# Context work placed between the latents' scan steps, lag blocks ahead of the chunk sums

## What is computed

```python
def token_mixer(h, h0_f, h0_b, rows, p):
    z = h @ p["w_in"]
    u, cb, cc, ch = jnp.split(z, [D_SSM, D_SSM + D_CONV, D_SSM + 2 * D_CONV], axis=-1)
    y_ssm, h_f, h_b = ssm_mixer(u, h0_f, h0_b, p)     # two complex diagonal scans, gelu, GLU
    y_conv = cb * short_conv(cc * ch, p["conv_w"], p["conv_b"], rows)
    y_ssm, y_conv = rmsnorm(y_ssm, ...), rmsnorm(y_conv per head, ...)
    return jnp.concatenate([y_ssm, y_conv], axis=-1) @ p["w_out"], h_f, h_b

def layer(x, cond, h0_f, h0_b, rows, p):
    sh1, sc1, g1, sh2, sc2, g2 = modulation(cond, p["w_mod"], p["b_mod"])
    y, h_f, h_b = token_mixer(rmsnorm(x, norm1) * (1 + sc1) + sh1, ...)
    x = x + g1 * y
    h = rmsnorm(x, norm2) * (1 + sc2) + sh2
    return x + g2 * peer(h, ...), h_f, h_b
```

## Time and profile before

| | us |
|---|---|
| median of three executions | 1924.85 |
| the profiled execution | 1922.27 |
| its span | 1920.1 |
| TensorE busy in the span | 1194.3 (62%) |
| VectorE busy | 1382.6 (72%) |
| ScalarE busy | 373.5 (19%) |
| GpSimd busy | 725.1 (38%) |
| HBM traffic, mean over the span | 396 GB/s |

### The profile page before, as it was taken

The page is one execution under the profiler, slowest core; times in us unless marked ns, Lnnn a source line. Parts: engine busy times, 40 slices in busy tenths (PEclk is TensorE's granted clock), DMA queues, the critical chain, the costliest instruction groups (busy, mean ns, idle before and its releaser), DMA issues.

```text
span 1920.1 us, 21154 instructions
## 1 busy us (share of the span) xinstructions
PE 1194.3 (62%) x7716; PEld 475.8 (25%) x7716; DVE 1382.6 (72%) x3664; ACT 373.5 (19%) x845; POOL 725.1 (38%) x666
## 2 busy tenths in 40 slices
PE   6989898999777777775543343544343454444434
PEld 3569644444322322221110000111000011111001
DVE  8968567777766766669777776677777678766664
ACT  5142441121122121111211110121111121111110
POOL 0000233344444434445434444444444354444440
PEclk9999999999878877775755555565555565555555
DMA  9855699999999999999999999999999999999994
GB/s 372 328 209 199 257 395 414 378 416 420 390 421 399 419 422 421 420 389 422 420 422 423 421 421 421 421 421 421 422 422 421 421 421 418 422 420 421 418 420 182
DMA packets 120968, 753.16 MB, mean 392 GB/s; under 512 B 12240, under 2 KB 27856, under 8 KB 33568
## 3 DMA queue, kind: packets, MB, share of 16 engines
q0 software_dynamic: 92160, 671.13, 84.5%
q1 hardware_dynamic: 28704, 80.69, 11.0%
HBM read 749.12 MB, written 11.04 MB: 396 GB/s over the span
## 4 chain that ended last, share of the span: by engine, by line
DMA 43%; PE 28%; DVE 23%; issue 2%; POOL 1%; ACT 1%; SPq 0%; DVEq 0%; POOLq 0%; ACTq 0%
DMA r<-table,gidx 31%; DVE r L1747 9%; DMA mix_r<-table,gidx 8%; PE bank L878 7%; PE bank L846 6%; PE bank L983 3%; DMA r<-w_mod 3%; DVE mix_r L1747 2%; PE bank L996 2%; PE bank L813 1%; POOL r L1935 1%; PE bank L962 1%; PE bank L855 1%; DVE i L1680 1%; PE bank L788 1%
## 5 line engine op out<-in xcount | busy, mean ns | idle before, releaser
L1935 POOL DMA_INDIRECT r<-table,gidx x542 | 607.7, 1121 | 865.3 <-PE bank L878 723.9
L1747 DVE CUSTOM_DVE_ANT_0 r<-r 128x1024 f32<-128x1024 f32 x542 | 658.1, 1220 | 246.5 <-DMA r<-table,gidx 246.0
L878 PE MATMUL bank<-r,cond 128*32 128x512 f32 x1432 | 327.2, 911 | 370.4 <-DVE cond L1759 295.2
L878 PE MATMUL bank<-r,wgt 128*32 128x512 f32 x736 | 166.8, 921 | 194.1 <-DVE wgt L1759 145.8
L1289 ACT ACTIVATE r<-r 128x2 f32<-128x2 f32 x320 | 65.1, 204 | 1013.1 <-DVE r L1747 1012.5
L878 PEld LDWEIGHTS bank<-r,cond 128*32 128x32 f32 x1432 | 37.1, 129 | 572.0 <-DVE cond L1759 437.2
L1935 POOL DMA_INDIRECT mix_r<-table,gidx x98 | 109.4, 1116 | 136.1 <-PE bank L878 117.0
L1747 DVE CUSTOM_DVE_ANT_0 mix_r<-mix_r,r 128x1024 f32<-128x1024 f32 x98 | 119.3, 1221 | 48.4 <-DMA mix_r<-table,gidx 48.2
L878 PE MATMUL bank<-mix_r,cond 128*32 128x512 f32 x264 | 91.1, 994 | 80.7 <-DVE cond L1759 63.4
L846 PE MATMUL bank<-hT_r,r 128*128 128x512 f32 x256 | 121.5, 630 | 0.9 <-ACT hT_r L1143 0.9
L878 PEld LDWEIGHTS bank<-r,wgt 128*32 128x32 f32 x736 | 18.9, 130 | 295.3 <-DVE wgt L1759 214.3
(11 more groups left out here) (367 smaller groups left out, 1637.1 us busy)
## 6 DMA issues: line engine op xcount, KB each, us to landing
r<-w_mod SPq DMA_DIRECT2D x24, 1024.0 KB, 9.7
r<-wq_heads SPq DMA_DIRECT2D x14, 1024.0 KB, 8.8
r<-table,gidx POOLq DMA_INDIRECT x542, 18.7
wq_heads<-w_query SPq DMA_DIRECT2D x8, 1024.0 KB, 12.1
r<-w_tiles SPq DMA_DIRECT2D x12, 512.0 KB, 7.8
x_r<-w_tiles SPq DMA_DIRECT2D x10, 512.0 KB, 6.0
hT_r<-xT SPq DMA_DIRECT2D x4, 640.0 KB, 6.1
r<-w_u SPq DMA_DIRECT2D x1, 2048.0 KB, 29.5
```

What stands on the lines that cost most here:

```text
L878: last = mm(bank[ACC[b % 2][h]][to:to + TG, :], pair_weights(NPR * G + g)[:, e, :], rows[SLOT[G * TOPK + k]][:, D + h * 512:D + (h + 1) * ...
L1747: V.tensor_tensor_reduce(row, row, h2r[tg], 1.0, 0.0, ALU.mult, ALU.add, hid[:, par, k:k + 1]).then_inc(dot_done, 1)
L1935: G_.indirect_dma_start(rows[SLOT[j]], None, table, bass.IndirectOffsetOnAxis(gidx[:, e, k:k + 1], 0)).then_inc(row_in[SLOT[j]], 16)
```

## The change

In the order of the kernel:

- **SP.** `load_mod(18)` and `(19)` stay, then come `load_conv_ctx(6)` and `(7)`, then the two `wt` loads, then `load_mod(20)` and `(21)`, `load_conv_ctx(8)` and `(9)`, `load_mod(22)` and `(23)`. The wait for `zc_mm` 2 ahead of `wt` goes.
- **PE.** The lag blocks' matmuls stand ahead of the chunk sums. Slabs 20 to 22 leave the selections of M; slab 20 stands behind `conv_ctx(0)`, which stands ahead of the context's scan outputs, and slabs 21 to 23 ahead of `conv_ctx(2)`. The GLU follows `conv_ctx(1)` and those slabs. The head sums and their spread come right behind it, `out_ctx` begins with the convolution's channels, and all eight `y_lat` stand between `scores(0)` and `spread_experts(0)`.
- **ScalarE.** Of chunk sums 8 to 15 it takes the even ones. The copy of `ccx` stands ahead of that of `Hbc`, the convolution's squares and root ahead of the GLU's sigmoid, the copy to `Hb` behind `take_scores(0)`.
- **VectorE.** It takes the odd chunk sums (`s_back`), copies the lag blocks ahead of the scan, and makes the imaginary products in one instruction with reversed halves instead of two. The context's convolution, norms and gating stand between the latents' steps (after steps 8, 11, 12, 14 and 15). Segment 2 follows them, segment 3 lies around the second root, and segment 4 comes after `xsc_ready`.

```diff
@@ sync @@
             for q in range(2):
                 load_conv_ctx(q)
-            for n in range(18, 24):
-                load_mod(n)
-            sp.wait_ge(zc_mm, 2)
+            load_mod(18)
+            load_mod(19)
+            for q in range(6, 8):
+                load_conv_ctx(q)
             for j in range(2):
                 sp.dma_start(wt[:, j, :, :], w_tiles[NCONV + j]).then_inc(wtg_in, 16)
-            for q in range(6, 8):
+            load_mod(20)
+            load_mod(21)
+            for q in range(8, 10):
                 load_conv_ctx(q)
+            load_mod(22)
+            load_mod(23)
             sp.wait_ge(m_mm, 2)
             sp.dma_start(wqa, w_query[:, :, 0:DQ]).then_inc(ld_first, 16)
-            for q in range(8, 10):
-                load_conv_ctx(q)
             sp.wait_ge(mod_mm, 24)
             sp.dma_start(woA, w_o[:, 0:4, :, :]).then_inc(ld_wo, 16)
             for q in range(10, 12):
@@ tensor @@
-            pe.wait_ge(bpt_ev, 17)
-            for g in range(16):
-                if g >= 2:
-                    pe.wait_ge(s_ev, g - 1)
+            def chunk_sums(g):
+
+                if g >= 10 and g % 2:
+                    pe.wait_ge(s_back, (g - 9) // 2)
+                elif g >= 2:
+                    pe.wait_ge(s_ev, min(g - 1, 4 + g // 2))
...
+            pe.wait_ge(bpt_ev, 17)
+            for g in range(8):
+                chunk_sums(g)
+            mod_slab(17)
+            for g in range(8, 16):
+                chunk_sums(g)
             mod_slab(18)
             mod_slab(19)
...
-                mod_slab(20 + a)
-            mod_slab(22)
...
+            pe.wait_ge(m_ev, 1)
+            conv_ctx(0)
+            mod_slab(20)
             pe.wait_ge(m_ev, 8)
             pe.wait_ge(hbc_ready, 1)
...
-            conv_ctx(0)
+            conv_ctx(1)
             pe.wait_ge(yc_gelu, 2)
...
+            mod_slab(21)
+            mod_slab(22)
             mod_slab(23)
-            conv_ctx(1)
+            conv_ctx(2)
...
             mod_turn(2)
-            conv_ctx(2)
+            head_sums()
+            spread_heads()
...
             pe.wait_ge(ld_wo, 32)
-            out_ctx(True, range(KS), 1)
-            out_ctx(False, range(KS, KD), 2)
+            out_ctx(True, range(KS, KD), 1)
+            out_ctx(False, range(KS), 2)
             pe.wait_ge(sqc_ready, 3)
             token_sums(257, sqx[0], True, False)
-            pe.wait_ge(hb_ready, 1)
-            pe.wait_ge(mod_free, 6)
-            y_lat(0, 0)
             pe.wait_ge(sqc_ready, 4)
             token_sums(257, sqx[1], False, True)
-            y_lat(0, 1, range(1))
             spread_root(1)
-            y_lat(0, 1, range(1, 5))
...
             first_query()
             scores(0)
-            y_lat(0, 2)
-            y_lat(0, 3)
-            for i in range(4):
-                y_lat(1, i)
+            pe.wait_ge(hb_ready, 1)
+            pe.wait_ge(mod_free, 6)
+            for n in range(2):
+                for i in range(4):
+                    y_lat(n, i)
             spread_experts(0)
@@ vector @@
-                link(tt(ta, prev, re, ALU.mult),
-                     tt(tb[:, :, 0, :], prev[:, :, 1, :], im[:, :, 0, :], ALU.mult),
-                     tt(tb[:, :, 1, :], prev[:, :, 0, :], im[:, :, 1, :], ALU.mult))
+                link(tt(ta, prev, re, ALU.mult), tt(tb, prev[:, :, ::-1, :], im, ALU.mult))
...
+            lag_blocks()
+            for g in range(9, 16, 2):
+                pr = g % 8 * 2
+                dve.wait_ge(s_mm, g + 1)
+                for r in range(2):
+                    src = bank[4 + g % 2][:, 0:4 * NCH].rearrange("p (q r c) -> p c r q", q=2, r=2)[:, :, r, :]
+                    V.tensor_copy(HH[:, NCC:0:-1, r, 1, pr:pr + 2], src[:, 0:NCC, :])
+                    last = V.tensor_copy(HH[:, NCH - 1:NCC:-1, r, 1, pr:pr + 2], src[:, NCC + 1:NCH, :])
+                last.then_inc(s_back, 1)
...
-                if i == 3:
-                    lag_blocks()
...
+            advance_rest(1, 9)
             dve.wait_ge(ccx_ev, 1)
             dve.wait_ge(zc_mm, 8)
...
+            advance_rest(9, 12)
+            dve.wait_ge(zc_mm, 12)
+            tt(mixc[:, KS:KD, :].rearrange("p k t -> p (k t)"), cvx.rearrange("p k t -> p (k t)"), bank[2][:, :], ALU.mult).then_inc(cvx_ev, 1)
+            advance_rest(12, 13)
...
+            residual_ctx(0)
+            residual_ctx(1)
+            segment_products(3)
             dve.wait_ge(rms_c, 3)
             V.reciprocal(inv1[1], rt1[1]).then_inc(inv_ready, 1)
             gains(4, COL_N2, 6)
+            segment_add(3)
+            segment_store(3)
             dve.wait_ge(inv_mm, 3)
...
             last.then_inc(xsc_ready, 1)
+            segment_products(4)
+            segment_add(4)
+            segment_store(4)
+            V.tensor_copy(small[:, 2:3], eps_c[:, :]).then_inc(scan_lat, 1)
```

More of the change, by code:

```diff
@@ L633, in _ @@
                 last.then_inc(s_mm, 1)
-                if g == 7:
-                    mod_slab(17)
             pe.wait_ge(bd_ready, 1)
@@ L647, in _, with conv_ctx @@
                 last.then_inc(k_mm, 1)
+            pe.wait_ge(bpt_ev, 17)
[4 more added lines that the diff above has]
+                chunk_sums(g)
             mod_slab(18)
             mod_slab(19)
+            def conv_ctx(r):
+                for i in range(4):
+                    q = 4 * r + i
+                    pe.wait_ge(wtc_in[WTC[q]], WTC[:q + 1].count(WTC[q]) * 16)
+                    for k in range(KD):
+                        last = mm(bank[r][:, i * P:(i + 1) * P], wtc[WTC[q]][:, k, :], hT[:, k, 0:CTX], start=(k == 0), stop=(k == KD - 1))
+                    last.then_inc(zc_mm, 1)
             pe.wait_ge(k_ev, 1)
-            pe.wait_ge(s_ev, 16)
+            pe.wait_ge(s_ev, 12)
+            pe.wait_ge(s_back, 4)
             for a in range(2):
@@ L1201, in _ @@
             act.wait_ge(bp_ready, 2)
-            for g in range(16):
+            for g in (*range(8), *range(8, 16, 2)):
                 d, pr = g // 8, (g % 8) * 2
@@ L1590, in _, with advance_rest @@
             rest = slice(1, NJ)
-            for i in range(1, SEG):
-                link(advance(seg[:, rest, i - 1, :, :], seg[:, rest, i, :, :], many_a, many_b, spread(AR, NJ - 1), spread(AI, NJ - 1)))
+            def advance_rest(lo, hi):
+                for i in range(lo, hi):
+                    link(advance(seg[:, rest, i - 1, :, :], seg[:, rest, i, :, :], many_a, many_b, spread(AR, NJ - 1), spread(AI, NJ - 1)))
             def segment_products(j):
```

95 lines of the change are left out of this document (39 added, 56 removed).

## The result

| | before | after |
|---|---|---|
| median of four executions, us | 1924.14 | 1961.3 |
| the profiled execution, us | 1922.27 | 1964.01 |
| its span, us | 1920.1 | 1962.2 |
| first gather issued, us | 215.58 | 254.73 |
| from there to the end of the span, us | 1704.5 | 1707.5 |

The kernel became slower by 37.2 us, estimated as a ratio of 1.0199 with an interval of 1.0181 to 1.0216 (the medians alone give 1.0193). Predicted were 1955, from 1938 to 1964, so the time lies in the range, near its upper end. In the profiled execution the first gather comes 39.15 us later; 30.5 were predicted. The sign and the main places were right, and the size was too small: by 6.7 us against the medians, and by 8.6 in the traces. The two differ because the profiled execution of after lies 2.7 us over the median of its four and that of before 1.9 us under its own.

The account below looks back on a forecast made before the run. The prediction took the DMA-bound expert stage to move with its first gather. That gather comes 30.5 us later, 23.8 before X and 6.7 behind; against the median of 1924.85 this gave 1955 us, range 1938 to 1964.

Parts of the forecast that it names:

- X: End of the scaling in the context's second normalisation, ahead of the key search: predicted at 223.6 us against 199.8 before.
- Lag blocks, chunk sums: Start of the context stage: lag matmuls first, VectorE sharing chunk sums; scan starts at 121.5 us instead of 117.5.
- the ceiling: Upper bound of 6.1 us for chunk-sum groups 8 to 15; the floor was 4.1 and the sum took 5.0.
- Lead and lag cancel: Context scan starts later but loses 3.1 us of lag copies and wait, so it ends at 136.8, where it ended before.
- the low end: Low case of the forecast's own range: faster landings, full clock and no gap, 18.7 us later, 1943.5 us.
- Merged products: Context scan on VectorE: one full-width product for two halves saves 0.06 us of a 0.98 us step.
- This decides: Loads moved on SP's queue: slab 20 issued at 140.6, landing at 148.0, so TensorE stands for 8.7 us.
- Behind X: From the second norm's scaling to the first gather: 22.5 us instead of 15.8, a new wait of 6.7 us.
- rival B: Half clock also behind X (4.4 us more), slab 20 landing in 10.9, groups 8 to 15 unchanged: 1964 us; chance 0.13.
- A: Rival: the loads TensorE waits for arrive in time; first gather 6.9 us later, 1931.8 us; chance 0.13.
- C: Rival: the expert stage gives time back, up to 22 us, for a faster kernel at 1910 us; chance 0.04.
- D: Rival: no effect, waits absorbed before X and the expert stage pays the rest, within 0.2%; chance 0.04.

Follow-up runs that it names:

- e8: Kernel before with only the lag blocks ahead of the chunk sums and the odd half of the last chunk sums on VectorE: 1926.85 us, ratio 1.0019.
- e7: Kernel before with only the merged imaginary products (one full-width product with reversed halves instead of two): 1921.81 us, ratio 0.9993.
- e2: Changed kernel with loads of slabs 20 to 23 and tiles 10 and 11 drawn ahead, mod_slab(21) moved next to mod_slab(20): 1943.54 us, ratio 1.0093.
- e4: Changed kernel with all 15 latents' steps ahead of the context's convolution, segments 2 to 4 behind it, and the copy to Hb early: 1954.94 us, ratio 1.0162.
- e11: Changed kernel with unread matmuls in four TensorE waits (ahead of slab 20, tile 10 and the first query, and behind its scores): 1955.65 us, ratio 1.0164.
- e3: Changed kernel with 36 unread matmuls of 128 columns in TensorE's wait ahead of mod_slab(20): 1960.74 us, ratio 1.0187.
- e5: Changed kernel with the edits of e2 and e4 together: 1946.76 us, ratio 1.0115.
- e9: e6 with VectorE's latent work cut up again: 13 steps ahead of the convolution, 2 behind, segments split around the product and root waits: 1930.91 us, ratio 1.0041.
- e6: e5 with two of the eight latents' outputs moved back between the token sums ahead of the first query: 1940.11 us, ratio 1.0090.
- e1: Changed kernel with slabs 20 and 21 loaded right behind slab 19, ahead of tiles 6 and 7: 1954.93 us, ratio 1.0155.

## Why the prediction was right in the main, and too small by 6.7 us

The table goes by the two traces, which have 8.6 us in the last line where the medians have 6.7.

| end of | predicted | after | later by |
|---|---|---|---|
| lag matmuls, chunk sums: scan starts | 121.5 | 123.2 | 1.7 |
| context scan | 136.8 | 138.2 | 1.4 |
| `conv_ctx(0)` | 139.3 | 143.2 | 3.9 |
| landing of slab 20 | 148.0 | 153.2 | 5.2 |
| `conv_ctx(1)` | 165.9 | 170.0 | 4.1 |
| slab 23 | 173.8 | 178.4 | 4.6 |
| `conv_ctx(2)` | 190.0 | 193.0 | 3.0 |
| start of the output product | 198.9 | 201.9 | 3.0 |
| its end | 214.8 | 219.0 | 4.2 |
| X | 223.6 | 227.8 | 4.2 |
| first gather | 246.1 | 254.7 | 8.6 |

*Lag blocks, chunk sums.* The lag matmuls took 3.70 us without a gap; a gap of 0.8 came in the chunk sums instead, and everything here lay 0.7 later from the start. Groups 8 to 15 took 6.0 us, so the ceiling held and VectorE's help bought nothing. The 5.0 in the sum had the earlier trace rows against it: groups 0 to 7, 128 records like these, took 5.54 us there without an idle time. "Lead and lag cancel" held in after within 1.4 us; e8 shows that in the order of before it isn't free (3.7 us). The sum had priced this part at nothing. Two slips of the working change little: VectorE's stretch "without a break" contains the 1.43 us of the earlier trace rows, which the sum does count, and the low end takes off 1.0 us for a gap of which the sum holds 0.8.

*Merged products.* A step took 0.91 us (0.92 predicted). Priced rightly, and worth next to nothing (e7).

*The loads.* "This decides" held for about half: e2 gives back 17.8 of 37.2 us. The issue (144.56) and landing (8.6 us for 7.4) give a wait of 9.96 for 8.7. The sum had 3.9 us for slab 23 and nothing for slab 22, and they cost 2.69 and 1.47: the same together. For tiles 10 and 11 the prediction names 10.6 us from the earlier trace rows, but its sum has 10.0 (174.3 to 184.3), and 9.1 came. Their wait was 3.89 for 6.7, also because tiles 8 and 9 ran slow in it: 1.6 us of half clock that cost nothing, since the load for which TensorE then waited had been issued at 178.8. VectorE's idle time, 18.43 us for 15, was seen.

*X.* The output product, the chain to it, and from its end to X (8.75 for 8.8) came out within 1.2 us. e4 confirms segment 3 at 1.8 us.

*Behind X.* 26.9 us for 22.5. That eight outputs and the copy to `Hb` stand between the scores and the spread was right, and VectorE waited 10.03 us there (10 predicted). The copy came at X + 7.1 rather than at X + 5.3: segment 4 was done at X + 4.9, but ScalarE takes the copy only after the first scores, and TensorE's first query took 6.64 us at half clock (3.81 in before). That is 1.8 us. The eight took 16.25 for 13.7, 2.5 us.

*The term that was too small is the clock's.* The prediction put half clock behind two long waits (4.4 us), left the first query and the latents' outputs to rival B, and had nothing for M and the output product. By after's rows against the same form at full clock it cost, on the path, 1.7 in M's second half, 2.0 in slab 20 and the outputs, 1.7 in tiles 10 and 11, 1.6 in the output product, 1.8 by the first query and 2.5 in the latents' outputs: 11.3. That is 6.9 more than counted, of the 8.6 in this trace. The other 1.7 are the rest of the terms together: the chunk sums ended 1.5 later and slab 20's landing took 1.2 more, and against that the landing of tiles 10 and 11 took 0.9 less. M's 1.7 are partly luck: in six of nine runs of this order M ran at full clock. e11 confirms part of the clock's cost by a run (4.6 us net at the first gather, 5.65 in time); for M and the output product, which it doesn't fill, it stays with the rows. And e3 shows that these losses don't simply add: behind them the next load may be what is late. The Trainium skill (TensorE: Matmul & The Clock Gate, HAM oscillation) says that an array which waits for each load comes back at half clock each time. This trace agrees behind the waits of 9.96 and 3.89 us for loads, but not behind that of 1.47 us, where slab 22 ran at full clock (1.07 us). It shows half clock behind short waits for other engines too, the last of them 1.31 us long.

*The rivals.* A fell: slab 20, slabs 22 and 23, and tiles 10 and 11 were all late. B came nearest, with 1964 for 1961.3. Its half clock behind X came (4.3 us for 4.4) and so did its unchanged groups 8 to 15; its landing of 10.9 didn't. So a good part of what it added was right, and it had 0.13 of the chance. C fell by the nearly constant last column of the table, and D with it, as X came 28 us later.

What stays open: why the short idle time before M's second half brings half clock in some runs and not in others (6.07 us in after, 5.95 in e2 and e3, 4.37 in the six other runs of this order, each behind the same 1.67), and what causes the "issue" gaps.

## What to carry to other kernels

Where loads are issued in one order by one queue, place a load by what its queue waits for ahead of it, not by where its data is needed: one that stands behind a wait for the matmuls just before its use is late by a whole landing. Idle time of an engine that another's delay has made isn't a place for work; once the delay is mended, the work put there is in the way (e5), and has to be cut into pieces again (e9). And small work that looks as though it only fills a gap may be what keeps TensorE at full clock for the step behind it (e6, e11).

## What the runs showed of the hardware

Adding dead matmuls made a kernel faster by 5.65 us (e11). Waits of 1.3 to 1.7 us were followed by half clock in several places, though not each time: the output product in after and in e9 (behind 0.76 and then 1.31 us in after), the first query in e5, and M's second half in some runs. In streams of short matmuls there are gaps of 0.3 to 2.7 us without releaser, which wander from run to run (none in the context's outputs in after, 1.86 us in e1, 2.33 and 0.92 in e2, 2.68 in e6); comparisons of single rows across runs have that much noise. Operands read with reversed halves cost VectorE nothing (in after 0.42 us for 128x256, as for the product beside it without reversal). Products that start a group, put into unused columns of a bank with an open sum, left e3's output off by 0.13, relatively, and had no such effect in banks without one (e11). The Trainium skill (PSUM — Partial Sum Buffer, The four PSUM rules) says that the first matmul of a group clears the written marks of the whole bank for its partitions. What e3 and e11 show agrees with it; neither looks at the marks themselves.
